# Expert layer: the first product of 46 of 64 groups as seven block products, all seven in a row, ahead of the eight values blocks

## The reference

```
h = gelu(einsum('td,thkd->thk', xs, u[es]))       # first product
out = einsum('thk,thkd->td', gs * h, v[es])       # second product, the "values"
```

## Time and profile before

| | |
|---|---|
| median of three runs | 5195.99 us |
| the profiled execution, its own time | 5194.93 us |
| its span, first to last instruction | 5193.1 us |
| TensorE matmul busy in the span | 4775.3 us (92%) |
| VectorE, ScalarE busy | 3066.3 us (59%), 1673.3 us (32%) |
| expert stage, layer 1 and layer 2 | 1141 to 2582 us and 3727 to 5166 us |
| mean granted TensorE clock | 0.957 |

### The profile page before, as it was taken

One profiled execution on the slowest core, in us unless ns is written; L12 is line 12 of the kernel. 1 busy time (PEld: TensorE's weight loads), 2 busy tenths in 40 slices (PEclk: granted clock), 3 DMA queues, 4 the chain that ended last, 5 costly groups with the idle time before them and its releaser, 6 DMA issues. The chain is left out here.

```text
span 5193.1 us, 99748 instructions
## 1 busy us (share of the span) xinstructions
PE 4775.3 (92%) x39596; PEld 4592.7 (88%) x39596; DVE 3066.3 (59%) x6292; ACT 1673.3 (32%) x2569; POOL 356.5 (7%) x196
## 2 busy tenths in 40 slices
PE   8777996989999999999997779969999999999998
PEld 8556896989999999999995658959899999999998
DVE  2555398865555555547725563988655555555577
ACT  2333234862222222222223332248522222222222
POOL 0200252000000000000002002520000000000000
PEclk9888998999999999999998789989999999999999
DMA  3330122673333333325323301227733333333353
GB/s 104 122 149 23 68 83 73 190 229 130 119 119 125 127 127 119 119 107 182 122 92 142 121 25 65 89 67 213 231 126 119 119 119 119 119 119 119 115 195 123
DMA packets 391378, 632.06 MB, mean 122 GB/s; under 512 B 29256, under 2 KB 327776, under 8 KB 349408
## 3 DMA queue, kind: packets, MB, share of 16 engines
q1 hardware_dynamic: 389120, 620.75, 33.7%
q10 hardware_dynamic: 2016, 8.26, 0.4%
HBM read 526.53 MB, written 152.36 MB: 131 GB/s over the span
## 5 line engine op out<-in xcount | busy, mean ns | idle before, releaser
L268 PE MATMUL ex_op<-ex_ah,ex_vl 128*128 128x288 f32 x3584 | 1066.6, 298 | 6.8 <-DVE ex_acc L2421 6.4
L270 PE MATMUL ex_op<-ex_ah,ex_vh 128*128 128x288 f32 x3584 | 1058.0, 295 | 0.0
L269 PE MATMUL ex_op<-ex_al,ex_vh 128*128 128x288 f32 x3584 | 1056.4, 295 | 0.0
L2421 DVE TENSOR_TENSOR ex_acc<-ex_acc,ex_op 128x576 f32<-128x576 f32 x896 | 672.6, 754 | 549.6 <-PE ex_op L270 537.5
L268 PE MATMUL ex_hp<-x_hi,ex_ul 128*128 128x288 f32 x3072 | 906.9, 295 | 20.0 <-PEq L124 17.0
L270 PE MATMUL ex_hp<-x_hi,ex_uh 128*128 128x288 f32 x3072 | 907.9, 296 | 0.0
L269 PE MATMUL ex_hp<-x_lo,ex_uh 128*128 128x288 f32 x3072 | 906.9, 295 | 0.0
L268 PEld LDWEIGHTS ex_op<-ex_ah,ex_vl 128*128 128x128 f32 x3584 | 674.4, 188 | 14.3 <-DVE ex_acc L2421 14.3
L270 PEld LDWEIGHTS ex_op<-ex_ah,ex_vh 128*128 128x128 f32 x3584 | 674.1, 188 | 0.0
L269 PEld LDWEIGHTS ex_op<-ex_al,ex_vh 128*128 128x128 f32 x3584 | 673.2, 188 | 0.0
L2370 ACT ACTIVATE ex_vh<-ex_v 128x2048 fp32r<-128x2048 f32 x128 | 245.6, 1919 | 1139.6 <-PE ex_op L270 860.6
(11 more groups left out here) (422 smaller groups left out, 8772.8 us busy)
## 6 DMA issues: line engine op xcount, KB each, us to landing
ex_u<-in_peer_uT SPq DMA_DIRECT2D x128, 1024.0 KB, 7.6
ex_v<-in_peer_v SPq DMA_DIRECT2D x128, 1024.0 KB, 6.8
gate_matrix<-g_stage SPq DMA_DIRECT2D x18, 4096.0 KB, 15.9
ex_g<-gate_matrix SPq DMA_DIRECT2D x128, 576.0 KB, 4.9
dec_k<-in_cache_kT SPq DMA_DIRECT2D x16, 1536.0 KB, 10.5
dec_v<-in_cache_v SPq DMA_DIRECT2D x16, 1536.0 KB, 8.4
out_s_k<-in_cache_k_kept SPq DMA_DIRECT2D x128, 190.5 KB, 6.2
out_s_v<-in_cache_v_kept SPq DMA_DIRECT2D x128, 190.5 KB, 6.2
```

What stands on the lines that cost most here:

```text
L268: nc.tensor.matmul(out, w_lo, x_hi, start=first, stop=False)
L269: nc.tensor.matmul(out, w_hi, x_lo, start=False, stop=False)
L270: return nc.tensor.matmul(out, w_hi, x_hi, start=False, stop=last)
L2421: nc.vector.tensor_tensor(a, a, o[:, :, 0:HALF], ALU.add).then_inc(s.added, 1)
```

## The change

The first product of a group is a product of a 2x2 block matrix (2 expert halves x 2 halves of the width) with a 2x2 block matrix (2 halves of the width x 2 halves of the tokens). For 46 groups (NQ, all that have a first product here but the first two) it is made by Strassen's scheme in Winograd's form: seven block products for eight. A block product is 4 width blocks x 3 passes = 12 matmuls of the same form as before, 84 a group for 96.

- The x side: four sums of blocks of x are made once a layer by VectorE and split (`high_x`, `low_x`).
- The u side: VectorE makes four sums of blocks of u (`sum_u`) a group, and seven blocks are split, each 512 elements a partition (`high_u` on ScalarE, `low_u` on VectorE).
- The result: four PSUM banks A, B, C, D; products 5 to 7 add onto A, C, A. ScalarE copies A after product 1 (`kept_p1`), D and C after product 4 (`kept_p45`) and A after product 5 (`kept_u2`), before TensorE adds onto them again; TensorE waits for these copies ahead of products 5, 6 and 7. VectorE makes three sums of a bank and a kept copy (`c_made`), to which gelu is applied in SBUF in three pieces.
- The order: on TensorE all seven products of a group, then the eight values blocks of the group before. On VectorE and ScalarE the steps are written out anew; v is split in four pieces of two blocks, into one buffer instead of two.
- Buffers: u and the gates have one buffer instead of two, v lies in the tile of h, whose 2.36 MB are parked in DRAM in the stage ahead (`parked_h`) and read back among the late groups. `acc` is no longer zeroed: the first add is a copy.
- The late groups: the adds now stand between the gate products and the low parts (`late_step`).
- 32 semaphores in the stage for 20, and one more in the stage ahead.

The diff, cut to its core; the lines taken out are those of the functions printed above, and what is left out besides is allocation, the ScalarE side of the opening and of the late steps, and loops like those before.

```diff
@@ -2208,6 +2208,8 @@
                                  ).then_inc(h_stored[f % 2], 16)
                 load(0)
+                sp.dma_start(m.parked_h[:, 0:4], m.h[:, 0:4]).then_inc(s.h_parked, 16)
+                sp.dma_start(m.parked_h[0:TS_, 4], m.h[0:TS_, 4]).then_inc(s.h_parked, 16)
                 for w in range(NU):
                     load(w + 1)
...
+    KH = KD // 2
+    A, B, C, D_ = (0, 0), (0, 1), (1, 1), (1, 0)
+    SLOTS = (("u", 0, 0), ("u", 0, 1), ("s", 0), ("u", 1, 1), ("s", 1), ("s", 3), ("s", 2))
+    BANKS = (A, B, C, D_, A, C, A)
+    OPENS = (True, True, True, True, False, False, False)
     with ExitStack() as ctx:
...
+                def next_loads(g, j):
+                    sp.wait_ge(s.ul, 7 * g - 3)
+                    load_u(g + (EARLY + 2))
+                    load_v(g + 1, g + (EARLY + 1), 1 - j)
+                    load_gates(g + 1, g + (EARLY + 1))
+                def late_loads(g, f):
+                    if f == 0:
+                        sp.wait_ge(s.ul, 7 * NQ)
+                    elif f == 1:
+                        sp.wait_ge(s.c_made, 3 * NQ)
+                    else:
+                        sp.wait_ge(s.gated, EG * (g - 1))
+                    sp.dma_start(early[f % 2], m.early_h[f].rearrange("p (e t) -> p e t", e=EG)
+                                 ).then_inc(early_in[f % 2], 16)
+                    load_v(g, f, f % 2, late=True)
+                    load_gates(g, f)
+                load_u(EARLY + 1)
+                load_v(0, EARLY, 0, True)
+                load_gates(0, EARLY, True)
+                load_v(1, EARLY + 1, 1, True)
+                sp.wait_ge(s.opened_ul, 1)
+                load_u(EARLY + 2)
+                load_gates(1, EARLY + 1)
...
+                def product(q, i):
+                    pe.wait_ge(s.ul, q * 7 + (i + 1))
+                    w_hi, w_lo, (x_hi, x_lo) = slot(m.u_hi, i), slot(m.u_lo, i), moving[i]
+                    for k in range(KH):
+                        ins = three_passes(nc, bank(BANKS[i]), w_hi[:, k], w_lo[:, k], x_hi[:, k], x_lo[:, k],
+                                           OPENS[i] and k == 0, k == KH - 1, not OPENS[i])
+                    ins.then_inc(s.product, 1)
+                def values(g, j, n, out, ring=2, first=False):
+                    if n == 0:
+                        pe.wait_ge(s.al, g * EG + EG)
+                    if n % 2 == 0:
+                        pe.wait_ge(s.vl, g * 4 + (n // 2 + 1))
+                    if not first:
+                        pe.wait_ge(s.added, g * KD + (n + 1 - ring))
+                    for half in range(2):
+                        t = slice(half * HALF, (half + 1) * HALF)
+                        c = slice(n * P, (n + 1) * P)
+                        for e in range(EG):
+                            ins = three_passes(nc, out[:, half, 0:HALF], v_hi[:, e, c], v_lo[:, e, c],
+                                               a_hi[:, j, e, t], a_lo[:, j, e, t], e == 0, e == EG - 1)
+                    ins.then_inc(s.out_made, 1)
+                def step(g, q, j, first=False):
+                    if first:
+                        pe.wait_ge(s.opened_gelud, 2 * EG)
+                    else:
+                        pe.wait_ge(s.c_made, q * 3)
+                    for i in range(4):
+                        product(q, i)
+                    pe.wait_ge(s.p1_kept, q + 1)
+                    product(q, 4)
+                    pe.wait_ge(s.p45_kept, q + 1)
+                    product(q, 5)
+                    pe.wait_ge(s.u2_kept, q + 1)
+                    product(q, 6)
                     for n in range(KD):
...
+                def late_values(g, j, first=False):
                     for n in range(KD):
...
+                def high_u(q, i):
+                    act.wait_ge(s.product, q * 7 + (i - 6))
+                    if SLOTS[i][0] == "s":
+                        act.wait_ge(s.s_made, q * 4 + (SLOTS[i][1] + 1))
+                    copy(slot(m.u_hi, i), source(i), s.uh)
...
+                def step(g, q, j, turn, last=False):
+                    high_v(g - 1, 1 - j, 3)
+                    act.wait_ge(s.product, q * 7 + 1)
+                    copy(kept_p1, bank(A), s.p1_kept)
                     if not last:
+                        act.wait_ge(s.u_in, g * 16 + 16)
+                        high_u(q + 1, 0)
+                        high_u(q + 1, 1)
+                    gelu(q, 0, a_raw[:, 0, lo_t])
+                    if not last:
+                        high_u(q + 1, 2)
+                        high_u(q + 1, 3)
+                    act.wait_ge(s.product, q * 7 + 4)
+                    copy(kept_p45, hp[:, 1, :, 0:HALF], s.p45_kept)
+                    act.wait_ge(s.product, q * 7 + 5)
+                    copy(kept_u2, bank(A), s.u2_kept)
+                    if not last:
+                        high_u(q + 1, 4)
+                        high_u(q + 1, 5)
+                    gelu(q, 1, a_raw[:, 0, hi_t])
+                    if not last:
+                        high_u(q + 1, 6)
+                    gelu(q, 2, a_raw[:, 1, :])
+                    high(g, j, 0, 0)
+                    high_v(g, j, 0, turn)
+                    high(g, j, 1, 1)
+                    high_v(g, j, 1)
+                    high_v(g, j, 2)
...
+                def step(g, q, j, last=False, first=False):
+                    add(g - 2, 7, first=first)
                     if not last:
+                        dve.wait_ge(s.u_in, g * 16 + 16)
+                        sum_u(q + 1, 0)
+                        sum_u(q + 1, 1)
+                        low_u(q + 1, 0)
+                    dve.wait_ge(s.p1_kept, q + 1)
+                    dve.wait_ge(s.product, q * 7 + 2)
+                    nc.vector.tensor_tensor(a_raw[:, 0, lo_t], kept_p1, bank(B), ALU.add).then_inc(s.c_made, 1)
+                    low_v(g - 1, 1 - j, 3)
+                    if not last:
+                        low_u(q + 1, 1)
+                        sum_u(q + 1, 2)
+                        sum_u(q + 1, 3)
+                        low_u(q + 1, 2)
+                        low_u(q + 1, 3)
+                        low_u(q + 1, 4)
+                    dve.wait_ge(s.u2_kept, q + 1)
+                    dve.wait_ge(s.product, q * 7 + 6)
+                    nc.vector.tensor_tensor(a_raw[:, 0, hi_t], kept_u2, bank(C), ALU.add).then_inc(s.c_made, 1)
+                    if not last:
+                        low_u(q + 1, 5)
+                    dve.wait_ge(s.p45_kept, q + 1)
+                    dve.wait_ge(s.product, q * 7 + 7)
+                    nc.vector.tensor_tensor(a_raw[:, 1, :].rearrange("p (a t) -> p a t", a=2),
+                                            bank(A).unsqueeze(1).to_broadcast([P, 2, HALF]), kept_p45,
+                                            ALU.add).then_inc(s.c_made, 1)
+                    if not last:
+                        low_u(q + 1, 6)
+                    add(g - 1, 0)
+                    dve.wait_ge(s.g_in, g * 16 + 16)
+                    dve.wait_ge(s.gelud, q * 3 + 2)
+                    gate(0, a_raw[:, 0, :])
+                    add(g - 1, 1)
+                    low(g, j, 0, 0)
+                    add(g - 1, 2)
+                    dve.wait_ge(s.gelud, q * 3 + 3)
+                    gate(1, a_raw[:, 1, :])
+                    add(g - 1, 3)
+                    low(g, j, 1, 1)
+                    low_v(g, j, 0)
+                    add(g - 1, 4)
+                    low_v(g, j, 1)
+                    add(g - 1, 5)
+                    low_v(g, j, 2)
+                    add(g - 1, 6)
+                def late_step(g, j, f_turn, first=False):
+                    add(g - 2, 7, not first)
+                    low_v(g - 1, 1 - j, 3, late=not first)
+                    dve.wait_ge(s.g_in, g * 16 + 16)
                     dve.wait_ge(early_in[j], f_turn * 16 + 16)
...
+                    low_v(g, j, 2, late=True)
+                    add(g - 1, 6, True)
+                nc.vector.tensor_tensor(acc[:], m.x_hi[:].bitcast(F32), m.x_lo[:].bitcast(F32), ALU.add
+                                        ).then_inc(s.x_made, 1)
+                dve.wait_ge(s.x_made, 1)
+                x11, x12, x21, x22 = (acc[:, k, t] for k in (k1, k2) for t in (lo_t, hi_t))
+                for out, a, b, after in ((x11, x12, x11, 0), (x12, x22, x12, 0), (x22, x22, x11, 1), (x21, x21, x22, 3)):
+                    if after:
+                        dve.wait_ge(s.t_made, after)
+                    nc.vector.tensor_tensor(out, a, b, ALU.subtract).then_inc(s.t_made, 1)
+                dve.wait_ge(s.opened_uh, 1)
+                nc.vector.tensor_tensor(m.u_lo[1][:], u_raw[:], m.u_hi[1][:].bitcast(F32), ALU.subtract
+                                        ).then_inc(s.opened_ul, 1)
+                def low_x(n, nth):
+                    dve.wait_ge(s.th, nth + 1)
+                    nc.vector.tensor_tensor(x_t[n][1], x_sum[n], x_t[n][0].bitcast(F32), ALU.subtract
```

(52 more changed lines are left out.)

375 lines of the change are left out of this document (198 added, 177 removed).

## The result

The changed kernel takes 5036.33 us (median of 4 runs, 5033.30 to 5040.98), the kernel before 5196.92 us beside it (4 runs): a ratio of 0.9696, 95% interval 0.968 to 0.9711. The forecast was 5049 us, faster, in a range of 5025 to 5092: the sign is right and the time lies in the range, 13 us under the forecast.

What follows compares the result with a forecast made beforehand. TensorE was taken as the bound, its time being matmul count by distance of starts. From 5194.9 us: -146.4 matmuls, +9 sixth product, +8 opening, -18.4 late groups, +1.5 barriers gave 5048.6, forecast 5049, range 5025 to 5092.

Steps and rivals of the forecast that it cites:

- The bound and the price of a matmul: Expert loop: TensorE never idles; 12 matmuls fewer in each of 92 groups, at 0.1326 us between starts, save 146.4 us.
- The sixth product: Loop: its wait for ScalarE's copy of C and D, in time by 0.14 us; 0.10 a group taken, 9 us.
- VectorE's place and load: Loop: VectorE needs 18.6 of 23.87 us a group, 78%; fifth add ends at 20.41, seventh values block due at 20.69.
- The opening: Stage start: TensorE idles about 4.6 us for the first add, then half clock; 13.2 us for 4.7, 8 more.
- The late groups: Stage end: adds placed between VectorE's other work win back 9.2 us a layer, 18.4 us in all.
- DMA and the SP queue: Single-buffered loads and parking and reading back h: taken as nothing, up to 3 us a layer.
- Barriers: 13 more semaphores to clear a layer: 0 to 3.3 us, 1.5 taken.
- Hand-offs bind: Rival, loop: product 6 and the seventh values block each miss by 0.28 us a group; 5091 us, chance 0.11.
- VectorE paces: Rival, loop: VectorE's instructions don't overlap, 25.0 us a group, only 42 us saved; 5144 us, chance 0.06.
- Slower by the clock: Rival: idle time ahead of product 6 drops the clock in each group, 176 us slower; 5355 us, chance 0.04.
- Busy time as the price: Rival: each matmul removed saves its 0.29 us busy time, 320 us in all; 4875 us, chance 0.02.

Runs made afterwards that it cites:

- copy_late_1: Changed kernel with ScalarE's fourth u piece made once more in each group, ahead of the copy of C and D for the sixth product; 5114.70 us.
- dve_values: Changed kernel with one more 512-column VectorE instruction in each group, between the adds of the values blocks; 5105.42 us.
- open_order: Changed kernel with VectorE's first adds in the opening moved ahead of three low parts of u and the second group's gates; 5032.67 us.
- late_adds_alone: Kernel before, with only VectorE's order in the late groups changed to that of the changed kernel; 5174.79 us, ratio 0.9957 to before.
- open_copy: Changed kernel with VectorE's first adds earlier in the opening and ScalarE's copy of C and D ahead of the fourth u piece; 5034.89 us.
- dve_products: Changed kernel with one more 512-column VectorE instruction in each group, placed where VectorE is idle in the products; 5045.35 us.
- six_products: Changed kernel with the second and fourth product of each group over half their depth, twelve matmuls fewer a group; 4893.79 us.
- copy_late_4: Changed kernel with ScalarE's fourth u piece made four times more in each group, ahead of the copy of C and D; 5350.88 us.
- eighth_product: Changed kernel with product 4 of each group made twice, so each group is back at 192 matmuls; 5194.59 us.

## Why the prediction was right, point by point

**The bound and the price of a matmul: right.** -146.4 us were predicted. Putting as many matmuls back cost 147.1 us of the expert stages, taking as many again away gave 145.4. The mean distance in the loop rose from 0.1326 to 0.1327 (1160 / 8748 and 1040 / 7835); by the unrounded values that is 0.024 us a group, 2 us in all.

**The sixth product: the term that was mis-sized.** The step took 0.10 us a group, +9 us, "since the margin is there but thin". No wait of TensorE in the loop names a copy, and the product's first matmul starts 0.13 us behind the one ahead in each of the 92 groups, so the term is nothing beside the 2 us above. Its due times were right: the fourth piece starts 6.55 us behind the first product's start (1716.13) for 6.57, the product is due at 7.95 for 7.96. But the copy ends at 7.72 for 7.82, because ScalarE's instructions overlap as well: the piece lasts 0.64 and the next starts 0.54 behind it, where 0.60 had been taken for both, and the copy lasts 0.63 for 0.65. The Trainium skill has this on its page ScalarE: Activation LUTs (What ACT_TABLE_LOAD costs): back-to-back ACTIVATEs overlap by about 93 ns; the 0.10 here agrees, and the prediction had passed it by. The hand-over, 0.13 us by copy_late_1, hadn't been counted at all; the two errors nearly cancel and leave 0.10 of margin. That is luck: with the prediction's own 7.82 and this hand-over the product could have started at 7.95, with nothing to spare. With a due time met, the term should have stood at zero and its bound in the range. The prediction had overlap for VectorE from rows 3 and did not look for it on ScalarE. This is 7 of the 13 us.

**VectorE's place and load: right in the place, low in the load.** The fifth add was to start at 19.65 and end at 20.41 behind the first product's start; it does at 19.67 and 20.41. Load was to be 78%, the window shows 83%; the sum took an overlap of 0.08 off every instruction, and one that starts behind idle time, as the add at 1709.95 behind 0.17 us, has none; in the loop's window that is 13 of a group's 30. The seventh block's margin was given as 0.28, without a hand-over; it is 0.24, and dve_values shows what lies behind it.

**The opening: right.** Predicted was an idle time of 4.6 us a layer and 1.7 at half the clock, 6.6 with the next adds; the wait is 4.7, the window behind it has clock 0.52. Its size is in part luck: in layer 1 the first add ends 35.9 us behind TensorE's start for 34.8, and the third block is due at 31.2 for 30.3, since more of the first product ran at half the clock. Against before the loss rises from 5.1 and 3.7 (14.4 and 13.0 less the 9.3 of the late groups) to 9.0 in both layers: +9.2 for the +8 predicted (13.2 less 4.7 is 8.5). Of the 9.2, 1.0 is the start of the stages at half the clock (1.6 and 2.4 us lost there in before, 2.5 and 2.5 in after), so that the opening itself costs 8.2. open_order shows the cause, VectorE's order.

**The late groups: right.** -18.4 predicted; 18.7 by late_adds_alone, and no idle time in the windows of after. The read-back of h wasn't felt.

**DMA and the SP queue: right.** They were put at nothing. No wait of TensorE in the expert stages names a transfer, and in the loop of layer 1 none of VectorE or ScalarE does.

**Barriers.** TensorE's wait at the stage's end grew from 2.5 (rows 9) to 3.1 us, 1.2 for two layers, against +1.5. What else the semaphores cost can't be told from the scatter of the stages around.

**The sum by these.** -146.4 + 2 - 18.7 + 9.2 = -153.9 in the expert stages, where the traces have -153.6. The predicted terms without the barriers make -147.8. The profiled execution thus came out 7.6 us below the sum's 5048.6, at 5041.0; the remaining 5 us to the median are the spread of the runs (the changed kernel has a median of 5036.33 beside before, and of 5044.24 beside open_copy).

**The rivals.** Hand-offs bind: no miss occurred, though the margins of 0.10 and 0.2 us show that it was close; what a miss costs isn't a fixed 0.28 but the whole delay past the margin and 0.1 for the matmul behind, 0.59 in dve_values and 0.74 in copy_late_1. VectorE paces: refuted by dve_products and six_products. Slower by the clock: with the copy 2.7 us late, copy_late_4 takes 5350.88 us. That is near the 5355 given for this rival (its own terms add up to 5362), but by another sum: a longer idle time, and half as many falls. In the changed kernel the copy was in time, so the rival's condition never came. Its point of decision, between 1.1 and 1.9 us, does not hold as a rule: 45 idle times of 2.6 us kept the clock. Busy time as the price: refuted by eighth_product.

## What to carry to other kernels

Where one engine runs without a gap, price a removed instruction by the distance of starts, and give the other engines not a load but a list of due times: an added instruction cost 0.59 us a group or nothing, by its place alone. A hand-off that meets its due time costs nothing even with a margin of 0.1 us; look for overlap on every engine before paying for it. What a large change leaves on the table is found where the loop starts and ends: reordering VectorE's late groups gave 18.7 us without the new scheme, and reordering its opening another 9.4 with it.

## What the runs showed of the hardware that was not expected

- The granted clock fell behind 45 of 90 equal idle times of some 2.6 us (copy_late_4). In the openings, idle times by the distance of starts, it fell behind 2.0 us (before, layer 1) and 4.9 (after) and stayed behind 1.3 (before, layer 2) and 1.2 (late_adds_alone, open_order).
- VectorE at 87% of a window held up nobody (six_products); in dve_values, at 83%, one instruction more did.
- From the end of ScalarE's copy to the first matmul that waits for it passed 0.13 us (copy_late_1), from the end of VectorE's add 0.06 (dve_values).
- Without an edit there, the stretch between the two expert stages took 1142.3 to 1151.1 us in the profiles, as much scatter as the opening was worth.
